# Input rows laid out turned in DRAM as well, so that the first left operands need no TensorE transposes

## The reference, cut to what matters

```
h = rms_norm(x, norm1_g[0])          # x: 256 x 1024
z = h @ w_in[0]                      # w_in: 1024 x 8704, the first matmul of the program
...
for i in range(2):                   # second block
    h = h + mixer(...) ; h = h + mlp_or_experts(...)
    gate = sigmoid(rmsnorm(h, ple_norm[i]) @ ple_gate[i])
    h = h + gate * (p[i] @ ple_proj[i])          # p[i]: 256 x 256
```

## Time and profile before

| | |
|---|---|
| device time, median of 3 runs | 2416.2 us (2416.17 to 2416.26) |
| device time of the profiled execution | 2416.35 us |
| its span (first to last instruction of the trace) | 2415.0 us |
| TensorE busy | 2387.8 us, 99% |
| VectorE, ScalarE, GpSimd busy | 1761.6, 1493.5, 86.5 us |
| moved by DMA | 612.42 MB |
| start of piece 0's first matmul (L761) | 8.84 us |
| DMA engines first less than 90% busy after their start | 43 us |

### The profile page before, as it was taken

How to read it: one execution, slowest core, us unless ns; L and a number is a source line. 1 busy time by engine, 2 the same in 40 slices (tenths; PEclk the granted TensorE clock), 3 DMA queues, 4 the chain that set the end, 5 groups by cost and what they waited for, 6 DMA issues and landing times.

```text
span 2415.0 us, 30624 instructions
## 1 busy us (share of the span) xinstructions
PE 2387.8 (99%) x12156; PEld 2016.8 (84%) x12156; DVE 1761.6 (73%) x2181; ACT 1493.5 (62%) x1955; POOL 86.5 (4%) x106
## 2 busy tenths in 40 slices
PE   9999999999999999999999999999999999999998
PEld 8888899888888998888888788888888888888887
DVE  6755655566466556565456579999999999999997
ACT  6355544444555445654446667777777777777775
POOL 0000000000000000100000200000000000000001
PEclk9999999999999999999999999999999999999999
DMA  8454565554446555355454379999999999999992
GB/s 309 142 173 140 168 251 192 175 174 151 164 139 202 192 175 170 110 178 192 155 194 157 122 269 390 395 393 379 382 381 385 377 385 379 383 379 377 384 385 98
DMA packets 268416, 612.42 MB, mean 254 GB/s; under 512 B 12472, under 2 KB 17958, under 8 KB 268268
## 3 DMA queue, kind: packets, MB, share of 16 engines
q1 hardware_dynamic: 263788, 594.71, 69.0%
q0 software_dynamic: 4320, 15.49, 1.6%
q10 hardware_dynamic: 160, 0.20, 0.0%
HBM read 599.59 MB, written 11.01 MB: 253 GB/s over the span
## 4 chain that ended last, share of the span: by engine, by line
PE 93%; DVE 5%; ACT 1%; POOL 1%; issue 1%; DMA 0%; DVEq 0%; ACTq 0%; POOLq 0%
PE PS L780 24%; PE PS L782 24%; PE PS L781 23%; PE PS L839 3%; PE PS L835 3%; PE PS L837 2%; DVE WL L2260 2%; PE PS L768 1%; PE PS L761 1%; PE PS L763 1%; PE PS L1383 1%; PE PS L882 1%; PE PS L891 1%; PE PS L996 1%; PE PS L965 1%; PE PS L1218 1%
## 5 line engine op out<-in xcount | busy, mean ns | idle before, releaser
L2260 DVE TENSOR_TENSOR WL<-raw,WH 128x1024 fp32r<-128x1024 f32 (+2 forms) x796 | 930.4, 1210 | 293.8 <-ACT WH L1677 289.0
L1677 ACT CAST WH<-raw 128x1024 fp32r<-128x1024 f32 (+2 forms) x796 | 792.5, 1042 | 326.8 <-PE PS L782 282.3
L780 PE MATMUL PS<-WH,XTH 128*128 128x512 f32 (+2 forms) x1952 | 771.8, 395 | 0.1
L782 PE MATMUL PS<-WH,XTL 128*128 128x512 f32 (+2 forms) x1952 | 755.2, 387 | 0.0
L781 PE MATMUL PS<-WL,XTH 128*128 128x512 f32 (+2 forms) x1952 | 753.7, 386 | 0.0
L782 PEld LDWEIGHTS PS<-WH,XTL 128*128 128x128 f32 x1952 | 366.6, 188 | 76.0
L780 PEld LDWEIGHTS PS<-WH,XTH 128*128 128x128 f32 x1952 | 367.0, 188 | 73.4 <-issue 2.7
L781 PEld LDWEIGHTS PS<-WL,XTH 128*128 128x128 f32 x1952 | 367.4, 188 | 69.0
L2260 DVE TENSOR_TENSOR WL<-AR,WH 128x1024 fp32r<-128x1024 f32 x334 | 391.6, 1221 | 26.9 <-ACT WH L1677 26.0
L1677 ACT CAST WH<-AR 128x1024 fp32r<-128x1024 f32 x334 | 334.2, 1052 | 66.0 <-PE PS L782 65.9
L780 PE MATMUL PS<-WH,HTH 128*128 128x512 f32 x706 | 275.0, 390 | 1.6 <-issue 1.6
(11 more groups left out here) (354 smaller groups left out, 1966.8 us busy)
## 6 DMA issues: line engine op xcount, KB each, us to landing
raw<-in_w_in SPq DMA_DIRECT2D x91, 1024.0 KB, 5.1
raw<-in_moe_w_gate SPq DMA_DIRECT2D x57, 1024.0 KB, 7.8
raw<-in_moe_w_up SPq DMA_DIRECT2D x57, 1024.0 KB, 8.0
AR<-in_moe_w_down SPq DMA_DIRECT2D x57, 1024.0 KB, 8.1
AR<-in_moe_w_gate SPq DMA_DIRECT2D x55, 1024.0 KB, 7.7
AR<-in_moe_w_up SPq DMA_DIRECT2D x55, 1024.0 KB, 7.9
raw<-in_moe_w_down SPq DMA_DIRECT2D x55, 1024.0 KB, 8.1
raw<-in_w_up SPq DMA_DIRECT2D x32, 1024.0 KB, 5.5
```

The source lines that it names most:

```text
L780: pe.matmul(o, lh, rh, start=start, stop=False, skip_group_check=True)
L782: return pe.matmul(o, ll, rh, start=False, stop=stop, skip_group_check=True)
L1677: act.copy(WH[:, i % WR, c], slots[s][:, c]).then_inc(*wh.inc(i, h))
L2260: dve.tensor_tensor(WL[:, i % WR, c], slots[s][:, c], WH[:, i % WR, c].bitcast(F32), ALU.subtract).then_inc(*wl.inc(i, h))
```

## The change

The host gives two more inputs: `x_turned` (1024 x 256, x transposed) and `norm1_col` (128 x 8, the first norm's weight as columns); `p_2` is given transposed in place of its old form.
- SyncE loads `x_turned` in two halves of 512 KB to a new tile `XR` (scratch that is free at that time) in the places where the two halves of x were loaded; the identity isn't loaded ahead of them. x itself, 1 MB in one DMA, and the identity are loaded after piece 1 and before piece 2.
- ScalarE and VectorE make `XTH` and `XTL` of the first norm from `XR`. The 16 transposes of x and the one of `G0` with its copy are gone. `norm` waits for the new, later load of x (`ld_n`).
- GpSimd sets a tile `WAKE` to ones first of all; TensorE starts with 13 real fp32 matmuls on it in place of the 22 idle transposes, without waiting for a DMA. ScalarE's first, dummy, activation reads `WAKE` as well.
- p needs no transposes: `ple_high` and `ple_low` make `PTH` and `PTL` from `PP` in SBUF, at the places of the old rounds.

```
 sync
-            sp.dma_start(CF[:, 0:128], cf[:, 0:128]).then_inc(ld_i, 16)
-            sp.dma_start(X[:, :, 0:512], xv[:, :, 0:512]).then_inc(ld_x, 16)
+            sp.dma_start(XR[:, 0:4, :], xv[:, 0:4, :]).then_inc(ld_x, 16)
             first_in = slots[HOME[0][0]].rearrange("p (k n) -> p k n", k=4)
             sp.dma_start(first_in[:, 0:2, :], PIECES[0][1][:, 0:2, :]).then_inc(ld_h, 16)
             sp.dma_start(first_in[:, 2:4, :], PIECES[0][1][:, 2:4, :]).then_inc(ld_w[HOME[0][0]], 16)
-            sp.dma_start(X[:, :, 512:1024], xv[:, :, 512:1024]).then_inc(ld_y, 16)
+            sp.dma_start(XR[:, 4:8, :], xv[:, 4:8, :]).then_inc(ld_y, 16)
...
+                    if j == 2:
+                        sp.dma_start(X[:, :, :], dr["x"][0].rearrange("(t p) d -> p t d", p=P)).then_inc(ld_n, 16)
+                        sp.dma_start(CF[:, 0:128], cf[:, 0:128]).then_inc(ld_i, 16)
 gpsimd
+            pool.memset(WAKE, 1.0).then_inc(*woke.inc(0))
             pool.memset(HALF[:, :], -0.5)
 tensor
-            pe.wait_ge(ld_i, 16)
-            pe.wait_ge(ld_g0, 16)
-            pe.transpose(PS[:, 7, 0:8], G0, ident[0:8, 0:8]).then_inc(*gt.inc(0))
-            free[7] = gcol.at(0)
-            awake(14)
-            half(("n1", 0), X, 0, ((ld_x, 16), None))
-            awake(8)
+            pe.wait_ge(*woke.at(0))
+            for _ in range(13):
+                pe.matmul(PS[:, 2, 0:P], WAKE, WAKE, start=True, stop=True)
...
                         if begins and k == 2:
-                            early()
                             pe.wait_ge(*wh.at(i, 1))
...
-                half(("pt", 0), PP, 0, ((ld_p[0], 16), None), 0, 2)
...
-                    half(("pt", 1), PP, 0, ((ld_p[1], 16), None), 0, 2, b0=0)
 scalar
-            act.dma_start(G0, dr["norm1_g"][0].rearrange("(c p) -> c p", p=P)).then_inc(ld_g0, 16)
-            act.wait_ge(ld_i, 16)
-            act.activation(sm[:, 252:253], ident[:, 0:1], ACT.Copy, scale=ident[:, 0:1])
-            act.wait_ge(*gcol.at(0))
-            for r in range(2):
-                half(("n1", 0), 0, gain4(("n1", 0), 0), only=(r,))
-                split(0, r)
-            half(("n1", 0), 1, gain4(("n1", 0), 1), b0=0)
+            act.dma_start(G[:, NG:NG + 8], dr["norm1_col"]).then_inc(ld_g0, 16)
+            act.wait_ge(*woke.at(0))
+            act.activation(sm[:, 252:253], WAKE[:, 0:1], ACT.Copy, scale=WAKE[:, 0:1])
+            act.wait_ge(ld_g0, 16)
+            for h, r in ((0, 0), (0, 1), (1, 0), (1, 1)):
+                if r == 0:
+                    act.wait_ge(ld_y if h else ld_x, 16)
+                for c in range(4 * h + 2 * r, 4 * h + 2 * r + 2):
+                    m = act.activation(XTH[:, c, :], XR[:, c, :], ACT.Copy, scale=gc(("n1", 0), c))
+                m.then_inc(*xh.inc("n1", 0, h, r))
+                if h == 0:
+                    split(0, r)
             split(1, 0)
             split(1, 1)
-            norm(("n1", 0), (ld_x, 16), (ld_y, 16))
+            norm(("n1", 0), (ld_n, 16), (ld_n, 16))
...
+            def ple_high(l):
+                act.wait_ge(ld_p[l], 16)
+                act.copy(PTH[:, :, :], PP).then_inc(*xh.inc("pt", l, 0, 0))
 vector
+            for h, r in ((0, 0), (0, 1), (1, 0), (1, 1)):
+                dve.wait_ge(*xh.at("n1", 0, h, r))
+                for c in range(4 * h + 2 * r, 4 * h + 2 * r + 2):
+                    m = dve.scalar_tensor_tensor(out=XTL[:, c, :], in0=XR[:, c, :], scalar=gc(("n1", 0), c),
+                                                 in1=XTH[:, c, :].bitcast(F32), op0=ALU.mult, op1=ALU.subtract)
+                m.then_inc(*xl.inc("n1", 0, h, r))
+                if h == 0:
+                    split(0, r)
...
+            def ple_low(l):
+                dve.wait_ge(*xh.at("pt", l, 0, 0))
+                dve.tensor_tensor(PTL[:, :, :], PP, PTH[:, :, :].bitcast(F32), ALU.subtract).then_inc(*xl.inc("pt", l, 0, 0))
```

More of the change, by code:

```diff
@@ L449, in program @@
                  for r in range(1 if k[0] == "pt" else 2)]
-        tx, xh, xl = sig("tx", turns), sig("xh", turns), sig("xl", turns)
+        tx = sig("tx", [k for k in turns if k[0] != "pt" and k[:2] != ("n1", 0)])
+        xh, xl = sig("xh", turns), sig("xl", turns)
         NORMS = [("n1", 0), ("n2", 0), ("n1", 1), ("n2", 1), ("nf", 0), ("pn", 0), ("nm", 1), ("nf", 1), ("pn", 1), ("last", 0),
@@ L789, in blocks, with group @@
                 return [w[:, k, c] for k in range(w.shape[1])]
-            def group(key, n, nk=2, k0=0, banks=(4, 5), early=None):
+            def group(key, n, nk=2, k0=0, banks=(4, 5), early=False):
                 for i, kp, t in lane.up(key, nk):
                     a, b = piece(i)
-                    begins = early is not None and (kp, t) == (0, 0)
+                    begins = early and (kp, t) == (0, 0)
                     if t == 0:
@@ L884, in half @@
                     free[b0 + r] = xl.at(*key, h, r)
-                    if key[0] != "pt":
-                        turned[2 * h + r] = xh.at(*key, h, r), xl.at(*key, h, r)
+                    turned[2 * h + r] = xh.at(*key, h, r), xl.at(*key, h, r)
             def heads(src, b, wd=P):
@@ L896, in gains @@
                 bank(7)
[L897 to L898 removed]
+                pe.transpose(PS[:, 7, 0:NG], GR[0:NG, :], ident[0:NG, 0:NG]).then_inc(*gt.inc(0))
+                free[7] = gcol.at(0)
                 yield
@@ L1063, in awake @@
                     pe.transpose(PS[:, 2, 0:P], ident, ident)
-            pe.wait_ge(ld_i, 16)
-            pe.wait_ge(ld_g0, 16)
-            pe.transpose(PS[:, 7, 0:8], G0, ident[0:8, 0:8]).then_inc(*gt.inc(0))
-            free[7] = gcol.at(0)
-            awake(14)
-            half(("n1", 0), X, 0, ((ld_x, 16), None))
-            awake(8)
+            pe.wait_ge(*woke.at(0))
+            for _ in range(13):
+                pe.matmul(PS[:, 2, 0:P], WAKE, WAKE, start=True, stop=True)
+            for c in range(4):
+                turned[c] = xh.at("n1", 0, c // 2, c % 2), xl.at("n1", 0, c // 2, c % 2)
             for l in range(2):
@@ L1076, in tensor @@
                         lane.until(("hgrn", l))
-                    rest = (lambda: half(("n1", 0), X, 1, ((ld_y, 16), None), b0=0)) if (l, g) == (0, 0) else None
-                    for kp, t in group(("in1", l, g), 512, early=rest):
+                    for kp, t in group(("in1", l, g), 512, early=(l, g) == (0, 0)):
                         if (l, g, kp, t) == (1, 0, 0, 0):
@@ L1253, in retention @@
                 yield
-            def ple_turn():
-                for _ in range(6):
-                    yield
-                half(("pt", 0), PP, 0, ((ld_p[0], 16), None), 0, 2)
             def ple_product():
@@ L2024, in ple_turn @@
                     yield
-                half(("pt", 0), 0, [None] * 2, PTH, 2)
+                ple_high(0)
             def ple_product(j):
@@ L2184, in scalar @@
                 if l:
-                    half(("pt", 1), 0, [None] * 2, PTH, 2, b0=0)
+                    ple_high(1)
                 for n in range(2):
@@ L2818, in ple_turn @@
                     yield
-                half(("pt", 0), 0, [None] * 2, PTH, PTL, 2)
+                ple_low(0)
             def begin(task):
@@ L3101, in vector @@
                 if l:
-                    half(("pt", 1), 0, [None] * 2, PTH, PTL, 2, b0=0)
+                    ple_low(1)
                 for n in range(2):
@@ L3245 @@
         a = np.ascontiguousarray(inputs[name])
-        if name in ("x", "p_2"):
+        if name == "x":
             a = np.ascontiguousarray(a[..., ORDER, :])
+        if name == "p_2":
+            a = np.ascontiguousarray(a[:, 0, ORDER, :].transpose(0, 2, 1))
         arrays[f"in_{name}"] = a
+        dr[name] = nc.dram_tensor(f"in_{name}", a.shape, mybir.dt.from_np(a.dtype), kind="ExternalInput").ap()
+    for name, a in (("x_turned", arrays["in_x"][0].T), ("norm1_col", arrays["in_norm1_g"][0].reshape(8, P).T)):
+        a = arrays[f"in_{name}"] = np.ascontiguousarray(a)
         dr[name] = nc.dram_tensor(f"in_{name}", a.shape, mybir.dt.from_np(a.dtype), kind="ExternalInput").ap()
```

22 lines of the change are left out of this document (11 added, 11 removed).

## The result

The changed kernel takes 2423.16 us (median of 10 executions, 2421.16 to 2424.38), the kernel before 2416.32 (10 executions, 2415.74 to 2417.3): a ratio of 1.0027, 95% interval 1.0019 to 1.0035, slower by 6.8 us, 0.3% and clear of noise. The forecast was 2416.9 with a range up to 2419.7.

The account below looks back on a forecast made before the run. TensorE, busy 99% of the 2415.0 us span, was taken as the bound. Waiting at piece 2 (+1.6 us) and p's removed transposes (-0.9) sum to +0.7, giving 2416.9 us against the median, with a range up to 2419.7.

Parts of the forecast that it names:

- Only D passes a bound: Whole kernel: of all cases, only D leaves the no-change band of 2411.4 to 2421.0 us; slower got 0.04.
- D: Rival at the two `XR` loads: 1 KB rows cost as much as 2 KB rows, +7.3 us, 2423.5; chance 0.03.
- All its later work is behind that: TensorE after piece 2: everything later moves with piece 2's delay of +1.6 us.
- x ahead of piece 2: Load queue: x's 1 MB delays piece 3's load, cast and eviction; TensorE begins piece 2 at 22.95, +1.6 us.
- Piece 5: Load of piece 5: lands 2.25 us later at 31.6, bank 4 free at 34.35, needed at 34.8; hidden.
- The start: First loads and pieces 0 and 1: first matmul near 7.75, 1.1 us earlier; piece 1 ends at 19.9, 1.2 earlier.
- B: Rival at piece 2: TensorE's own start decides, the eviction waits for no load; 2413.9 us, chance 0.08.
- The rate of loading: Load queue: extra megabyte costs 2.7 us at the trace's 389 GB/s; the skill's fit says 2.4, first turned half at 3.9.
- The warm-up: TensorE's start: 13 matmuls take 1.4 to 2.8 us, end by 3.9; possible half clock is covered, cost zero.
- C: Rival after TensorE's 3 us wait at piece 2: the clock falls, half clock costs 2.7 us; 2419.6, chance 0.13.
- p: Two rounds of four p transposes, one per layer, between back-to-back matmuls: 0.46 us each, -0.91 us together.
- E: Rival at the p turnings: they are hidden and give nothing back, 2417.8 us; chance 0.76 together with the main case.

Follow-up runs that it names:

- a_pad5: The changed kernel with 18 in place of 13 warm-up matmuls, 20 more instructions ahead on TensorE: 2417.15 us, ratio 1.0004 to the kernel before.
- a_less2: The changed kernel with 11 in place of 13 warm-up matmuls, 8 instructions fewer: 2419.2 us, ratio 1.0014 to the kernel before.
- b_fewer: The kernel before without its 22 idle transposes, 44 instructions fewer on TensorE, nothing else changed: 2423.17 us, ratio 1.003.
- a_pad64: The changed kernel with 77 in place of 13 warm-up matmuls, 256 more instructions ahead of the branch: 2429.52 us (one execution).
- a_padlate: The changed kernel with 10 more idle transposes (20 instructions) just ahead of the branch at the end: 2419.86 us, ratio 1.0012 to the kernel before.
- b_p_only: The kernel before with p turned on the host and its parts made from SBUF, 18 fewer instructions: 2415.24 us, ratio 0.9995.
- a_pad32: The changed kernel with 45 in place of 13 warm-up matmuls, 128 more instructions ahead of the branch: 2418.23 us (one execution).
- a_lazy2: The changed kernel with 18 warm-up matmuls and ScalarE's casts of pieces 3 and 5 after the evictions, a_lazy run again: 2414.21 us, ratio 0.9991.
- a_latex: The changed kernel with 18 warm-up matmuls, x loaded after piece 4, and norm's sum of squares from turned x (result not the reference's): 2416.94 us.
- a_lazy: The changed kernel with 18 warm-up matmuls and ScalarE's casts of pieces 3 and 5 after the evictions of g = 0 and 1: 2414.25 us.
- b_p_lazy: The kernel before with p turned on the host and casts of pieces 3 and 5 behind the evictions, no turned x: 2414.86 us, ratio 0.9994.

## Why the prediction was wrong

The forecast of the change's own parts held to half a microsecond; with the second pause taken out (a_pad5) the kernel takes 2417.15 where I had 2416.9. In part that is luck: the loads cost 0.34 us more than forecast (+1.94 for +1.6) and p gave back 0.18 more (1.09 for 0.91). The sum was incomplete.

- **The step that failed** is the bound "Only D passes a bound", and before it "All its later work is behind that": I let every shift run unchanged to the end and priced TensorE's instructions by what each of them takes, never by where their removal leaves the others. 46 fewer instructions moved a branch target, 970 us after the last edit, next to a fetch border: 2.45 us of pause and 1.71 of half clock in the profiled execution, 4.2 of the 4.8 by which the span grew (3.9 net). a_pad5 (gone with 20 more), a_less2 and b_fewer (moved by just the number of instructions taken out or left in, the last without anything of the change), and a_pad64 (back with 256 more) show it. The first pause of 1.56 us stood in the trace of before, put down to "issue"; I hadn't read it. It could have told me that the end depends on the instruction stream, though not that this change would strike the border; for that the instructions had to be counted.
- **x ahead of piece 2**, the main term: +1.41 for +1.6. XN at 14.46 (14.7), third cast at 20.04 (20.1), eviction 21.94 (22.0), piece 2 at 22.77 (22.95), TensorE idle 2.8 us (3).
- **Piece 5, "hidden, with 0.45 us to spare"**: not hidden. Its cast began at 32.31, not 31.6: the extra loads had moved it by 2.9 us, not 2.25. TensorE waited at piece 4, and the shift grew from 1.41 to 1.94 by 43 us. This was one of my signs of failing ("if a later wait takes up or adds to the shift"). A slack of 0.45 in a sum of five rows is none.
- **The start**: first matmul at 7.36 (7.75), end of piece 1 at 19.8 (19.9). The rows of 1 KB cost nothing that shows: x's first half was in use at 4.97, 0.2 before my estimate. D is refuted, and B, as the eviction decided. That D's 2423.5 lies beside the measured 2423.16 is chance: no part of its price was paid (and that price put piece 3's landing at 24.0, short of the 24.2 from which D was to decide).
- **The rate of loading**: the fit of the Trainium skill, "DMA: Bandwidth & Descriptors", that was set beside the term would have made x's megabyte cheaper still than the trace's rate did, and piece 5 moved by more than either; x's first half was in use at 4.97, not at 3.9. The page gives this fit for DMAs on GpSimd's path, which the prediction doesn't say; these loads are SyncE's.
- **The warm-up**: priced at half. 0.11 us was the time of one record, and an fp32 matmul of 128 columns shows as two ("x26" for 13 matmuls): 4.81 us, not 1.4 to 2.8. It ended at 5.8 and cost nothing, as forecast, with another cover: TensorE idled 1.57 us, not 4, and piece 0 ran at full clock. The price I gave for half clock (12 x 0.2 + 5.4/2 is 5.1, "no more than 3") didn't add up. b_fewer, whose first matmuls do run at half clock, begins piece 2 1.65 us late for it.
- **C, the clock**: given 0.13 as a whole. It holds in a part of the executions and is worth 1.4 us in a_less2's trace, not 2.7; the groups of one kernel lie 1.4 to 2.1 us apart. It is the likeliest reason why the median of the changed kernel, 2423.16, lies above its profiled execution, 2421.16; its two groups lie some 2.1 apart, so a longer end may be in it as well. With 13 warm-up matmuls about half of the executions are in the higher group (five or six of ten in the changed kernel, six in a_padlate), with 18 three of eleven (a_pad5).
- **p**: -1.09 in the trace (-0.52 and -0.57), -1.10 by b_p_only, for -0.91. E is refuted.
- **G0 and the constants**: nothing, as forecast.

Put together for the profiled execution: +1.41 + 0.53 - 1.09 = +0.85, and +3.9 at the end. The median has 2.0 us more, likely C's.

What stays open: why the first pause is 2.26 us in a_less2 and 1.0 in a_pad32 and a_lazy2; why the clock stays up behind a pause of 1.13 us and after some waits of 2.8, and falls after others of 2.9 and after one of 1.83 (a_latex).

## What to carry to other kernels

Where a kernel has a branch, count the instructions of the busiest engine before and after an edit: the stall behind the branch depends on where its target falls among blocks of 256, and a handful of idle instructions under a wait moved it for nothing. When a span changes, compare the start of the same instruction at five or six places down the trace before explaining anything; here the cost lay more than 2300 us behind most of the edits. And before a load is added to a full queue, look in each engine's stream for what stands behind the instruction that will wait for it: putting the eviction ahead of the cast was worth 2.9 us with the late load (a_pad5 to a_lazy), and 0.4 at most without it (b_p_only to b_p_lazy).

## What the runs showed that I had not expected

- Behind the taken branch TensorE stops for 1.5 to 1.8 us in most profiles (2.26 in one, 1.0 and 1.1 in two), and once more for 2.2 to 2.9 us where a border of instruction blocks lies 3 or 5 instructions further, 1.1 us where it lies 13 further, and not at all where it lies 133 (a_pad32), 215 (before), 233 (b_p_only) or 241 (a_pad5) further. The period of the border is 256 instructions (a_pad64), not 128 (a_pad32).
- After the long second pause the granted clock falls to 0.5 for about 3 us (0.52 from 2380 to 2383 us), which costs 1.7 us more.
- After a wait of 2.9 us at 20 us of the span the clock fell to 0.51 in a_less2's profile and stayed at 1.00 after waits of 2.8 in three others. The two groups of times of one and the same program suggest that it falls in a part of its executions.
- Turned rows of 1 KB land no later than rows of 2 KB at the start of the queue (in use 4.2 us after their issue; 4.5 to landing before, with the 64 KB identity ahead of them).
